# Weight loads of two groups in one 1 MB transfer, with one semaphore for two ring slots

## What is computed

```python
# block 1
z = rms_norm(x) @ w_in            # mLSTM and forgetting attention on z
x = x + mixed @ w_out
a, g = split(rms_norm(x) @ w_up)  # width 2 x 5632
x = x + (gelu(conv(a)) * g) @ w_down
x = x + sigmoid(rms_norm(x) @ w_ple_gate) * (p @ w_ple_proj)
# block 2
mod = silu(c) @ w_mod + b_mod     # six vectors of 2048, on VectorE
y = mixer(rmsnorm(x) * (1 + sc) + sh, w_in_2)      # convolution and gated linear attention
x = x + g_m * rmsnorm(y @ w_out_2)
u = conv(h @ w_up_2);  x = x + g_f * rmsnorm((silu(g) * val) @ w_down_2)
```

## Time and profile before

| | us |
|---|---|
| median of three runs | 2447.53 |
| the profiled execution, its own time | 2449.02 |
| span of the profiled execution | 2447.4 |
| TensorE busy | 2423.7 |
| VectorE busy | 1781.3 |
| ScalarE busy | 1161.0 |
| 512 KB weight loads, issue to landing, median | 4.4 to 4.6 |

### The profile page before, as it was taken

One profiled execution on the slowest core, in us unless ns is written; L12 is line 12 of the kernel. 1 busy time (PEld: TensorE's weight loads), 2 busy tenths in 40 slices (PEclk: granted clock), 3 DMA queues, 4 the chain that ended last, 5 costly groups with the idle time before them and its releaser, 6 DMA issues.

```text
span 2447.4 us, 35080 instructions
## 1 busy us (share of the span) xinstructions
PE 2423.7 (99%) x12856; PEld 2084.3 (85%) x12856; DVE 1781.3 (73%) x2396; ACT 1161.0 (47%) x1348; POOL 124.0 (5%) x230
## 2 busy tenths in 40 slices
PE   9999999999999999999999999999999999999998
PEld 7888888888888888888888888888888888888887
DVE  5878776698898897677656677777777777775444
ACT  6454455444444444444445445455544444444443
POOL 0000000001001000011002000000000000000000
PEclk9999999999999999999999999999999999999999
DMA  7878776688888888889764655576666666666665
GB/s 256 269 241 250 235 218 190 198 274 288 282 282 290 272 282 272 269 315 309 266 194 136 187 165 164 173 247 218 197 189 186 191 188 186 184 193 197 193 195 167
DMA packets 260929, 551.20 MB, mean 225 GB/s; under 512 B 17216, under 2 KB 18544, under 8 KB 260704
## 3 DMA queue, kind: packets, MB, share of 16 engines
q1 hardware_dynamic: 229344, 442.55, 56.9%
q0 software_dynamic: 28096, 102.82, 13.2%
q10 hardware_dynamic: 3392, 4.50, 0.6%
HBM read 547.68 MB, written 2.13 MB: 225 GB/s over the span
## 4 chain that ended last, share of the span: by engine, by line
PE 91%; DVE 4%; DMA 2%; ACT 1%; issue 1%; SPq 0%; DVEq 0%; POOLq 0%; ACTq 0%
PE PS L1859 35%; PE PS L1866 18%; PE PS L1814 11%; PE PS L1816 11%; PE PS L1815 11%; DMA mod_w<-in_w_mod_rows 2%; DVE w_lo L1104 1%; DVE mod_w L1084 1%; PE PS L2171 1%; ACT w_hi L581 1%; PE PS L1852 1%; DMA xr<-in_x 0%; PE PS L1917 0%; PE PS L1928 0%; PE PS L1935 0%
## 5 line engine op out<-in xcount | busy, mean ns | idle before, releaser
L581 ACT ACTIVATE w_hi<-w_raw 128x1024 fp32r<-128x1024 f32 x832 | 880.4, 1060 | 1097.5 <-PE PS L1866 558.9
L1104 DVE TENSOR_TENSOR w_lo<-w_raw,w_hi 128x1024 fp32r<-128x1024 f32 x832 | 1015.2, 1224 | 504.1 <-ACT w_hi L581 489.4
L1859 PE MATMUL PS<-xs,w_hi 128*128 128x512 f32 x3792 | 942.4, 393 | 0.0
L1859 PEld LDWEIGHTS PS<-xs,w_hi 128*128 128x128 f32 x3792 | 685.7, 189 | 125.8 <-issue 0.3
L1866 PEld LDWEIGHTS PS<-xs,w_lo 128*128 128x128 f32 x3840 | 515.8, 191 | 32.5
L1866 PE MATMUL PS<-xs,w_lo 128*128 128x256 f32 x3840 | 526.4, 282 | 0.0
L1814 PE MATMUL PS<-w_hi,hs 128*128 128x512 f32 x704 | 274.2, 389 | 0.0
L1816 PE MATMUL PS<-w_hi,hs 128*128 128x512 f32 x704 | 273.9, 389 | 0.0
L1815 PE MATMUL PS<-w_lo,hs 128*128 128x512 f32 x704 | 273.9, 389 | 0.0
L1084 DVE SCALAR_TENSOR_TENSOR mod_w<-mod_w,c_row 128x1024 f32<-128x1024 f32 x192 | 234.2, 1220 | 30.7 <-DMA mod_w<-in_w_mod_rows 30.2
L1814 PE MATMUL PS<-w_hi,xs 128*128 128x512 f32 x564 | 222.2, 394 | 5.6 <-DVE w_lo L1104 4.1
(11 more groups left out here) (301 smaller groups left out, 1387.3 us busy)
## 6 DMA issues: line engine op xcount, KB each, us to landing
w_raw<-in_w_up SPq DMA_DIRECT2D x352, 512.0 KB, 4.5
w_raw<-in_w_in SPq DMA_DIRECT2D x208, 512.0 KB, 4.4
mod_w<-in_w_mod_rows POOLq DMA_DIRECT2D x192, 512.0 KB, 6.3
w_raw<-in_w_down SPq DMA_DIRECT2D x176, 512.0 KB, 4.6
w_raw<-in_w_out SPq DMA_DIRECT2D x64, 512.0 KB, 4.5
w_raw<-in_w_ple_gate SPq DMA_DIRECT2D x32, 512.0 KB, 4.6
xr<-in_x SPq DMA_DIRECT2D x4, 512.0 KB, 8.7
w_raw<-in_w_ple_proj SPq DMA_DIRECT2D x4, 512.0 KB, 4.5
```

What stands on the lines that cost most here:

```text
L581: nc.scalar.activation(w_hi[:, slot, :, :], w_raw[:, slot, :, :], ACT.Copy).then_inc(hi_made, 1)
L1104: V.tensor_tensor(w_lo[:, slot, :, :], w_raw[:, slot, :, :], w_hi[:, slot, :, :].bitcast(F32), ALU.subtract).then_inc(lo_made, 1)
L1859: ins = M(PS[:, bank + b, :], w_hi[:, slot, k, b * P:(b + 1) * P], x(cs[k]), start=begin and k == 0, stop=end and k == GK - 1)
```

## The change

SP loads two groups that follow each other in one transfer of 1 MB, which fills two neighbouring slots. The wait ahead of it is that for the slot of the second group (`layer.group(i, s, j + 1) + 1`). The four `w_full` semaphores become two, one for a pair of slots, and ACT waits for the pair's semaphore ahead of either half. The two projection layers have one group for each strip; there SP issues both loads, waits itself until both have landed (`proj_full`), and raises the pair's semaphore. Splits, matrix products, sizes of the ring and the order of all other work stay.

```diff
-        return lambda i, s, j: w[:, GK * j:GK * j + GK, ...]
+        return lambda i, s, j: w[:, GK * j:GK * j + 2 * GK, ...]
...
+    def two_strips(w, first=0):
+        return lambda i, s, j: w[:, 0:GK, (first + s) * STRIP:(first + s + 1) * STRIP]
...
-    w_full = [sem(f"w_full{i}") for i in range(RING)]
+    w_full = [sem(f"w_full{i}") for i in range(RING // 2)]
...
                 def pair(i):
+                    if layer.G == 1:
+                        slot = layer.slot_int(i, 0, 0)
+                        sp.wait_ge(lo_made, layer.group(i, 1, 0) + 1)
+                        for s in range(2):
+                            sp.dma_start(w_raw[:, slot + s, :, :], source[name](i, s, 0)).then_inc(S["proj_full"], 16)
+                        sp.wait_ge(S["proj_full"], 32 if name == "proj1a" else 64)
+                        sp.sem_inc(w_full[slot // 2], 16)
+                        return
                     for s in range(2):
-                        for j in range(layer.G):
+                        for j in range(0, layer.G, 2):
...
-                            sp.wait_ge(lo_made, layer.group(i, s, j) + 1)
-                            sp.dma_start(w_raw[:, slot, :, :], source[name](i, s, j)).then_inc(w_full[slot], 16)
+                            sp.wait_ge(lo_made, layer.group(i, s, j + 1) + 1)
+                            sp.dma_start(w_raw[:, slot:slot + 2, :, :], source[name](i, s, j).rearrange("p (s k) n -> p s k n", s=2))\
+                                .then_inc(w_full[slot // 2], 16)
...
-                    act.wait_ge(w_full[slot], 16 * (g // RING + 1))
+                    act.wait_ge(w_full[slot // 2], 16 * (g // RING + 1))
```

More of the change, by code:

```diff
@@ L214, in plain @@
     def plain(w, first=0):
-        return lambda i, s, j: w[:, GK * j:GK * j + GK, ((2 * i + s) + first) * STRIP:((2 * i + s) + first + 1) * STRIP]
+        return lambda i, s, j: w[:, GK * j:GK * j + 2 * GK, ((2 * i + s) + first) * STRIP:((2 * i + s) + first + 1) * STRIP]
     def up(w):
-        return lambda i, s, j: w[:, GK * j:GK * j + GK, bass.ds(i * STRIP + s * D_FF, STRIP)]
+        return lambda i, s, j: w[:, GK * j:GK * j + 2 * GK, bass.ds(i * STRIP + s * D_FF, STRIP)]
     in1_strips = [(FOX0 + e * 1024 + f * STRIP, 32 + e * 8 + f * NB) for f in range(2) for e in range(3)] \
@@ L230, in listed @@
     def listed(w, strips):
-        return lambda i, s, j: w[:, GK * j:GK * j + GK, strips[2 * i + s][0]:strips[2 * i + s][0] + STRIP]
+        return lambda i, s, j: w[:, GK * j:GK * j + 2 * GK, strips[2 * i + s][0]:strips[2 * i + s][0] + STRIP]
     def out1_first(n):
@@ L241, in rows @@
             c = (GK * j + out1_first(n)) % KC
-            return w[:, c:c + GK, n * STRIP:(n + 1) * STRIP]
+            return w[:, c:c + 2 * GK, n * STRIP:(n + 1) * STRIP]
         return rows
+    def two_strips(w, first=0):
+        return lambda i, s, j: w[:, 0:GK, (first + s) * STRIP:(first + s + 1) * STRIP]
     source = {
@@ L247, in two_block_kernel @@
         "up1": up(w_up1),
-        "down1": plain(w_down1), "gate1a": plain(w_gate1), "proj1a": plain(w_proj1), "gate1b": plain(w_gate1, 2),
-        "proj1b": plain(w_proj1, 2), "in2": listed(w_in2, in2_strips),
+        "down1": plain(w_down1), "gate1a": plain(w_gate1), "proj1a": two_strips(w_proj1), "gate1b": plain(w_gate1, 2),
+        "proj1b": two_strips(w_proj1, 2), "in2": listed(w_in2, in2_strips),
         "out2": plain(w_out2), "up2": up(w_up2), "down2": plain(w_down2),
@@ L356, in two_block_kernel @@
     mod_used = sem("mod_used")
[L357 removed]
+    names = """gain_loaded proj_full par_loaded c_loaded gate_loaded gate2_loaded p_loaded gw2_loaded consts cleared pad2_zeroed masks_made
         x_turned cact_made row_sq y_sq var_made std_made hn_hi x_ready
@@ L576, in split_hi @@
                         return
-                    act.wait_ge(w_full[slot], 16 * (g // RING + 1))
+                    act.wait_ge(w_full[slot // 2], 16 * (g // RING + 1))
                 else:
-                    act.wait_ge(w_full[slot], i * (16 * 2 * layer.G // RING) + 16 * ((layer.g0 + s * layer.G + j) // RING + 2))
+                    act.wait_ge(w_full[slot // 2], i * (16 * 2 * layer.G // RING) + 16 * ((layer.g0 + s * layer.G + j) // RING + 2))
                 act.wait_ge(w_used, layer.group(i, s, j) + 1 + RING)
@@ L733, in _ @@
                 for slot in (2 * k, 2 * k + 1):
-                    act.wait_ge(w_full[slot], 16)
+                    act.wait_ge(w_full[slot // 2], 16)
                     act.wait_ge(w_used, slot + 1)
```

## The result

The changed kernel takes 2513.8 us in the median of four runs (2503.23 to 2516.73), the kernel before 2446.95 (2446.03 to 2447.6): a ratio of 1.0263 with a 95% interval of 1.0246 to 1.028. It is slower by 66.9 us. The forecast was 2452.6 and the range ended at 2470. The profiled execution took 2516.38 us.

The account below looks back on a forecast made before the run. The prediction took TensorE's matrix products as the bound (busy 2423.7 of 2447.4 us). Start 2.8, first `in1b` strips 0.3, `up1` 0.5 and `out2` 1.5 made 5.1 us: 2447.5 + 5.1 = 2452.6 us, range 2448 to 2470.

Parts of the forecast that it names:

- The undisturbed 1 MB landing: Time for a pair's load to land without other traffic: 4.8 us from below, 5.9 us from above.
- the link that the sum had priced: In `out2`: a load issued after both splits lands 9.4 us later, group 564 is late, 1.6 us lost.
- the sum: Whole kernel: 2.8 + 0.3 + 0.5 + 1.5 = 5.1 us added to the median.
- The start: Program start, where ScalarE has no reserve: TensorE loses 0.7 to 3.8 us, taken as 2.8.
- Its chain: At the start: group 4 1.3 us late, group 8's split 2.5 to 3.8, then the diagonal, then groups 10 and 11.
- The fourth link: At the start: groups 10 and 11 land beside `c_row` in 4.8 to 7.9 us; the copy costs TensorE 0.7 to 3.8.
- The steady stages: Loss of 0.5 us in `up1`; none in `in2`, `up2`, `down2`, the gates and `down1`.
- the third rival: Ring's turn becomes the limit in stages with `w_mod`: landing 7.0 us, whole kernel 2465 to 2490 us; chance 0.19.
- estimate of 4.4 us: Latency of two groups in one transfer, by the skill's 2.0 us fixed cost; 3.2 us each in two.
- The walk: One round of 16 groups followed in `up1`: no TensorE wait at 5.5 us landing, 12 us lost at 6.5.
- L: Time after the second group's split until its pair lands; tested in `up1`, limit near 6.2 us.
- The sign: Expected mark in `up1`: where VectorE's wait for ScalarE appears on every round; `up1` longer, TensorE waiting for `w_lo`.

Follow-up runs that it names:

- e12: The change, but with single loads for the first twelve groups of `out1` and for the projections: 2508.42 us (ratio 1.0259).
- e3: Against the kernel before: later request and common landing wait together, but as two 512 KB transfers with a semaphore each: 2512.84 us (1.0262).
- e4: The change with all but the first two `w_mod` tiles cut to 64 bytes per partition, VectorE's operation keeping its length: 2448.21 us (1.0007).
- e10: The change with the small `w_mod` tiles, and in `up1` a 64-byte load that SyncE waits for ahead of each pair: 2480.53 us (1.0133).
- e13: The change with half of each `w_mod` tile loaded (512 of 1024 columns), VectorE's work unchanged: 2458.77 us (1.0053).
- e11: The kernel before (single loads) with small `w_mod` tiles, and in `up1` the 64-byte load and wait ahead of even groups only: 2442.81 us (0.9983).
- e9: The change, but in `up1` the split of a strip's last position comes ahead of that strip's evacuation: 2497.6 us (1.0201).
- e5: The change with full `w_mod` tile loads, but VectorE reduces only 16 of a tile's 1024 columns: 2477.35 us (1.0119).
- e6: The change with 1 MB pairs only in layers without `w_mod` tiles (gates, `in2`, `up2`, `down2`), single loads elsewhere: 2447.48 us (1.0003).

## Why the prediction was wrong, step by step

The steps that held. The undisturbed 1 MB landing was bounded by 4.8 to 5.9 us and is 5.0 in the median of `up2`. `in2`, `up2` and `down2` lose nothing. `out2` lost 1.2 where 1.5 stood, which is partly luck: with the same pairs there e12 and e3 lose 3.7 and 2.6, and no trace was read for the link that the sum had priced. For the projections nothing (at most 0.5) was put down; SyncE waited 8.5 us there in two waits, and in e4, which keeps these waits, the stage takes 99.3 us.

The start was put at 2.8 us and lost 0.8. Its chain came true as far as the diagonal, each link a little early: ScalarE's split of group 4 was 0.8 us late instead of 1.3, the pair 8, 9 landed after 6.9 us (6.6 to 7.9), the diagonal ended at 32.97 (33.3 to 34.6), 2.2 us later than in the earlier trace rows, and TensorE waited for it:

```profile
32.49 0.48 DVE L1277 TENSOR_SCALAR mix<-ident,stat 128x128 f32<-128x128 f32 x2
...
35.84 0.42 DVE L1302 COPY mix<-PS 128x256 f32<-128x256 f32 x1
...
PE PS L1976 <- DVE mix L1277: 0.8, 1, 0.8
```

The fourth link failed here: groups 10 and 11, issued at 28.6, 1.2 us ahead of `c_row`, landed in 5.0 us, not in up to 7.9. The copy ended at 36.26 and TensorE, 0.8 us late itself, wanted it only at 35.86 + 0.8 = 36.7. Other executions with the same start lose 1.1 to 3.6 us in `in1a`; in e12, with 3.6, the wait for the diagonal was 2.0 us. So the size was within the scatter, but the last link, on which the sum had put it, cost 0.4 us at most with 1 MB pairs (e10), and 2.1 in e3.

The step that failed is **"The steady stages"**, in three places.

First, its input: "I take 5 to 6 us, nearest to the undisturbed rows, since pairs come half as often as groups". Beside tiles the landing is 6.7 us in `up1`. Half as many loads of twice the size are the same bytes beside the same tiles, so the earlier trace rows with 1.3 added for the second half, which the text had as 7.0 in the third rival, was the nearer row. The Trainium skill's rule for large transfers ("DMA: Bandwidth & Descriptors", section "Bandwidth") bore on nothing here: e3 with 512 KB and the change with 1 MB differ by 1 us, within their intervals. Its fixed cost, which the prediction used for an estimate of 4.4 us, is given for GpSimd's path; SyncE's 1 MB loads in `up2` took 4.8 us at least, and the measurement decides.

Second, its price. The walk gave 12 us at L = 6.5 and the rival 12 + 22 = 34 at 7.0, so about 20 at 6.7; `up1` lost 35.3, and 24.3 at least in the other kernels whose `up1` is paired like it. The walk gave every landing the same L. The trace's run from 4.9 to 9.5, and a turn with 8.4 beside an evacuation is 3.5 us too long at once, while a short one gives back little, since no more than four slots can lie ready. How the spread adds up was not worked out. e13 shows the other side: with 5.1 in the median a landing of 8.0 costs nothing.

Third, its reach. `down1` was put down at nothing for its "more reserve or fewer neighbours on VectorE" and lost 14.3 us, at a landing of 7.2 in the median. The test for L had been made in `up1` only. `in1b` (5.5) had 0.3 in the sum and the third rival's "add some". `out1` (6.2) was in no case: there ScalarE's queue turned a late load into a wait for an input.

What the runs show in its place: with four slots in pairs there are two turns under way instead of four, and each must hold landing, both splits and VectorE's other work within 11.2 us. Shown for `up1`: without long landings nothing is lost (e4), with a latency put in by hand 32 us are (e10), single slots take that latency (e11), and less work between the halves gives back 9 to 20 (e9). The sign was that of the third rival. Its upper end of 2490 had 34 us for `up1` and 8 for all the rest, where `in1b`, `down1`, the gates and `out1` lost 31.5.

Open: how the loss of `up1` divides between landing and VectorE's tiles (e5 takes a part of it away, but shortens the landings too); the turns of `down1`, for which no run was made by itself; why e3's start is 5.3 us slower; and a ring of six or eight slots, which wasn't tried: the kernel uses some 215 KB of each partition already.

No version beats the kernel before; e6 equals it. Faster, by less than 0.2%, were only kernels that leave out tile bytes.

## What to carry to other kernels

Before two slots of a small ring are tied together, write down the turn: issue, landing, every engine that must touch both slots, whatever stands between these in the engines' queues, and the next issue; compare it with the time in which the consumer uses the whole ring, in each stage, with the spread of the landings and not the median alone. A producer's waits for the consumer (here 558.9 us) look like a large reserve and are not one: they sum many short waits, and the tightest place has 2.5 us. Test two halves of a change together as well as apart, since near such a limit they don't add.

## What the runs showed of the hardware

After the stall of 5.07 us in `out1` TensorE came back at half speed. The windows 389 to 395, 395 to 400 and 400 to 405 us of the changed kernel (the clock is the third number from the end):

```profile
389.00:395.00 6.00, 1.11 (x5) 0.57 (x4) 4.24 (x6) 2.95 (x3) 0.00 (x0) 0.89 0.31 94
395.00:400.00 5.00, 4.81 (x11) 3.80 (x12) 2.31 (x3) 0.00 (x0) 0.00 (x0) 0.50 0.59 190
400.00:405.00 5.00, 5.00 (x22) 4.10 (x21) 2.79 (x3) 2.13 (x2) 0.00 (x0) 0.95 0.36 141
```

A granted clock of 0.50, the 1.2 GHz level, held until 400.4 us, where a matmul's length went from 0.63 to 0.39 us:

```profile
399.59 0.63 PE L1827 MATMUL PS<-w_lo,xs 128*128 128x512 f32 x1
...
400.71 0.39 PE L1827 MATMUL PS<-w_lo,xs 128*128 128x512 f32 x1
```

From 395.2 to 400.4 half of the time was lost, some 2.6 us beside the 5.07 of the stall. In e12, with a stall of 1.4 us in that stage, all of these windows stand at 1.00. It happened again at the start of the gates: TensorE was idle for 1.18 and 2.67 us, ahead of 1257.2 and 1262.9, and from 1264.4 to 1267.4 its matmuls took 0.63 us.

A 64-byte load with a wait for it holds SyncE's next load back by 1.7 us in the mean in e10, 1.3 at least (1.2 of them as a wait, 80.2 us in 66), and by 2.8 in e11. The 1.7 us are enough to move `up1` from no loss to 32 us.
